# Hybrid decoder block on one core: first expert pair's loads written out, and expert weights loaded through two DMA queues

## The chip, the cores and the metric

The kernel runs on one core of one Trainium2 chip. The metric is the device time in microseconds of one execution. TensorE (PE in the profile) does the matrix products, VectorE (DVE) and ScalarE (ACT) the elementwise work, SyncE (SP) issues DMA transfers. An engine that can issue DMAs does so through a queue of its own: in the profile SP's transfers are queue q1 and ScalarE's are queue q10.

## The reference, cut to what matters

```python
def hybrid_layer(x, ...):
    xn = rms_norm(x, norm1_g)
    u, q, k, v, qi, ki, wi, gs, ga = split(xn @ w_in)
    y_ssm = s5_mixer(u, ...)                       # diagonal state space model, scan over 256 tokens
    y_att = dsa_attention(rope(q), rope(k), v, rope(qi), rope(ki), wi)   # 64 keys chosen for each token
    mixed = sigmoid(gs + b0) * (y_ssm @ w_proj_ssm) + sigmoid(ga + b1) * (y_att @ w_proj_attn)
    x = x + mixed @ w_out
    return x + moe(rms_norm(x, norm2_g), ...)

def moe(h, ...):                                   # 256 tokens, 32 experts, 4 chosen for each token
    gates = softmax over the top 4 of (h @ w_router + b_router), zero elsewhere
    for e in range(32):
        z = h @ w_moe_in[e] + b_moe_in[e]          # 1024 x 2048
        zg, zl = min(z[:, ::2], 7), clip(z[:, 1::2], -7, 7)
        act = zg * sigmoid(1.702 * zg) * (zl + 1)
        out += gates[:, e] * (act @ w_moe_out[e] + b_moe_out[e])   # 1024 x 1024
```

Everything is float32. The output is the RMS norm of the block's result.

## The kernel before

**Stages.** First the mixer: norm, the combined projection, the state space model, the attention, the projections and the residual. Then the head of the expert stage (router, places of the tokens, gates). Then 32 experts, one after the other. Each engine runs its own program; semaphores join them. The order on each engine is written out by hand.

**Mixer.** TensorE works through jobs (`JOBS`) of two 128-column tiles each (`feature_job`, the matmul of L1038). A job writes one of two rotating PSUM banks (`rot`, banks 0 and 1, by the parity of its number in `JOBS`), and a bank is free again when the job before last has been evicted (`rot_free`). The jobs P0_0 and P0_1 are the transposed probabilities of the first 128 tokens. Weights come in chunks of 1 MB through four slots (`wbuf`), loaded by SP. `mean_between` puts the matmul that sums the squares between the halves of job U0. `round_` is one of four rounds of the state space model on VectorE: four products that read the PSUM banks 4 to 7 (the last raises `bu_used`), two sums, eight scans, four more products. `score_job` writes the same banks 4 to 7; the first one waits for `bu_used` 4, `roped` 3 and copies of the keys. `choose_keys` finds the 64 largest scores in eight steps of eight.

**Experts.** An expert has 12 MB of weights, in six chunks of 2 MB (`NT`): chunks 0 to 3 (`NT_IN`) are its input weights, chunks 4 and 5 its output weights. SBUF holds two experts (`place_of(half, n)`), so expert e+2 takes the place of expert e, chunk by chunk. `chunk_used` counts the chunks that TensorE has finished; `moe_in[half][n]` says that a chunk has arrived.

TensorE's `body` for one expert, in order: input matmuls for k = 0 to 7 (L1326; two k for each chunk, a wait for the chunk at each even k; bias matmuls of L1337 after k = 0, and for the second expert the output bias of L1342), scatter of the expert before (L1302), gather for the next (L1285), transposes (L1351, L1355, L1293), output matmuls (L1366; a wait for chunk 4 at the start and for chunk 5 half-way). ScalarE evicts the output sums at L570 (`y_tok`) when `chunk_used` shows that the whole expert is done.

**Loads of the experts.** All go through SP. The first two experts are loaded during the mixer (`load_first`). From then on `one_pass` of SP reads the token count (`most_tokens`, waits for `flag_ok`) and runs a loop over pairs: for each chunk in the order 0 to 5 it waits until TensorE has used the same chunk of the expert two before, and issues the load (L373). Last comes the load of the final gain (L376, 0.5 MB). The output is stored from L381.

Of the kernel before, what the change touches and what calls it, by code (L numbers as in the profile page):

```python
# [21 lines left out]
T = 256  # L22
# [33 lines left out]
        "A0", "A1", "A2", "GLU0", "GLU1", "P0_0", "P0_1", "A3", "PS0", "PS1", "PS2",  # L56
# [15 lines left out]
def build(nc, io, out):  # L72
# [3 lines left out]
    with ExitStack() as ctx:  # L76
# [119 lines left out]
        u0_first, w_gain, tok_ok, rpart_ok, scaled_ok = [sem(n) for n in ("u0_first", "w_gain", "tok_ok", "rpart_ok", "scaled_ok")]  # L196
        x_in = [sem(f"x_in{n}") for n in range(2)]
# [6 lines left out]
        turned1, turned1_out = sem("turned1"), sem("turned1_out")  # L204
# [91 lines left out]
        def _(sp):  # L296
# [8 lines left out]
            def load_first(*pairs):  # L305
# [5 lines left out]
            sp.dma_start(wbuf[:, 0, 0:1024], io["w_mix"][0, :, 0:1024]).then_inc(u0_first, 16)  # L311
            sp.dma_start(x1[:, 4:8, :], io["x_t"][:, 4 * T:8 * T].rearrange("p (k t) -> p k t", k=4)).then_inc(
                x_in[1], 16)
# [49 lines left out]
            def one_pass(c, first, most_tokens=None):  # L363
                if most_tokens:
                    most_tokens()
                with sp.Fori(1 if isinstance(c, int) else 0, NE // 2) as m:
# [27 lines left out]
        def _(ac):  # L394
            ac.dma_start(x1[:, 0:4, :], io["x_t"][:, 0:4 * T].rearrange("p (k t) -> p k t", k=4)).then_inc(
                x_in[0], 16)
# [22 lines left out]
            for n in range(2):  # L419
                ac.wait_ge(x_in[n], 16)  # L420
# [73 lines left out]
            def prob_turned(t):  # L494
                for n in range(2 * (t + 1)):
                    if t:
                        ac.wait_ge(turned1, n + 1)
                        ac.activation(prob_t[:, 512 * n:512 * n + 512], ps[:, 4 + n, :], ACT.Copy).then_inc(
                            turned1_out, 1)
                    else:  # L500
                        evict(f"P0_{n}", prob_t[:, 512 * n:512 * n + 512], lambda b: b)
# [52 lines left out]
            def one_pass(c, first, most_tokens=None):  # L554
# [4 lines left out]
                def body(j, tail=False):  # L559
# [10 lines left out]
                    ac.activation(y_tok, ps[:, 2, :], ACT.Copy).then_inc(y_tok_ok, 1)  # L570
                gathered_rows(first)
                body(first)
                if most_tokens:
                    most_tokens()
                with ac.Fori(1, NE - 1) as e:
                    body(e + first)
                body(first + NE - 1, tail=True)
# [19 lines left out]
        def _(ve):  # L597
# [25 lines left out]
            for n in range(2):  # L623
                ve.wait_ge(x_in[n], 16)
                for k in range(4 * n, 4 * n + 4):
# [92 lines left out]
            def round_(i):  # L718
# [6 lines left out]
                tt(prod[3], bre, ei, ALU.mult).then_inc(bu_used, 1)  # L725
                ve.wait_ge(bu_used, i + 1)
# [38 lines left out]
            round_(0)  # L765
            round_(1)
            round_(2)
# [43 lines left out]
            def mask(t, first, end):  # L811
# [4 lines left out]
                if t:  # L816
                    ve.wait_ge(rot_done, JOB["P0_1"] + 1)
# [198 lines left out]
        def _(pe):  # L1016
# [28 lines left out]
            def mean_between(step):  # L1045
                if step == 1:
                    pe.wait_ge(ones_ok, 1)
                    pe.wait_ge(sq_sum, 1)
                    pe.matmul(ps[:, 2, 0:T], ones, squares[:, 0, :], start=True, stop=True).then_inc(mean_done, 1)
                    chunk_arrived(pe, "U0")  # L1050
# [486 lines left out]
```

## Time and profile before

| | |
|---|---|
| median of 3 runs | 1152.15 us (1150.76 to 1152.37) |
| the profiled execution | 1152.06 us |
| its span in the profile | 1150.3 us |
| PE busy | 1107.7 us, 96% |
| DVE busy | 342.5 us, 30% |
| ACT busy | 156.1 us, 14% |
| read from HBM | 435.52 MB |
| mean rate of the DMA engines over the span | 381 GB/s |
| mean granted TensorE clock | 0.998 of full |

A share of busy time is an average over stages that have different limits: VectorE is busy nine tenths or more of the mixer's first half and one tenth of the expert stage. So the view by slices of the span comes first, then the order of work in each stage. In the views, "x8" is a number of instructions, "[1.65 <-issue]" is the idle time before an instruction and what ended it, and each matmul call in float32 stands as two instructions. Times are from the start of the span.

### The profile page before, as it was taken

Reading aid. Unit: us, or ns where it says so; the run is one execution under the profiler, and the core shown is the slowest. Engines: PE = TensorE matmul, PEld = TensorE weight load, DVE = VectorE, ACT = ScalarE, POOL = GpSimd, SP = SyncE. Lnnn points to the kernel's source line nnn. Section 1 sums busy time; section 2 is a strip of 40 time slices with the busy share of each in tenths; the row PEclk is TensorE's granted clock in tenths of the full one; section 3 lists DMA queues with packets and bytes.
Section 4 is the critical chain, followed back from the end, with each engine's and each line's share of the span. In section 5 each row is a group of like instructions: output and inputs, shape, how many; then the busy total and the mean of one; then the engine's idle time right before and its main releaser. Section 6 shows DMA issues by size and latency. Waiting matters only on the chain.

```text
span 1150.3 us, 13793 instructions
## 1 busy us (share of the span) xinstructions
PE 1107.7 (96%) x5564; PEld 484.2 (42%) x5564; DVE 342.5 (30%) x761; ACT 156.1 (14%) x330; POOL 0.7 (0%) x8
## 2 busy tenths in 40 slices
PE   9999999999999999999999999999999999999996
PEld 7887788833333333333333333333333333333332
DVE  7999982121221211111111111111111111111112
ACT  2411361220101000010000000000000000000002
POOL 0000000000000000000000000000000000000000
PEclk9999999999999999999999999999999999999999
DMA  8344577769999999999999999999999999999995
GB/s 336 133 157 142 195 313 284 312 266 430 426 428 428 428 428 428 428 428 428 428 428 428 428 428 428 428 428 428 428 428 428 428 428 428 428 428 428 428 428 231
DMA packets 34010, 437.73 MB, mean 381 GB/s; under 512 B 4032, under 2 KB 4160, under 8 KB 6080
## 3 DMA queue, kind: packets, MB, share of 16 engines
q1 hardware_dynamic: 33840, 436.84, 90.5%
q10 hardware_dynamic: 144, 0.52, 0.2%
q8 instruction: 19, 0.31, 0.1%
q14 instruction: 7, 0.06, 0.0%
HBM read 435.52 MB, written 1.05 MB: 380 GB/s over the span
## 4 chain that ended last, share of the span: by engine, by line
PE 66%; DMA 17%; SPq 5%; DVE 2%; ACT 1%; issue 1%; another core or an unknown queue 0%; ACTq 0%; DVEq 0%
PE ps L1326 28%; DMA mem<-in_w_moe 17%; PE ps L1366 15%; PE ps L1038 6%; SPq L373 5%; PE ps L1302 4%; PE ps L1285 4%; PE ps L1251 2%; PE ps L1337 2%; PE ps L1216 1%; PE ps L1293 1%; PE ps L1351 1%; PE ps L1127 1%; PE ps L1355 0%; DVE late L606 0%
## 5 line engine op out<-in xcount | busy, mean ns | idle before, releaser
L1326 PE MATMUL ps<-mem,late 128*64 128x512 f32 x2048 | 459.0, 596 | 24.5 <-DMA mem<-in_w_moe 23.7
L1326 PEld LDWEIGHTS ps<-mem,late 128*64 128x64 f32 x2048 | 142.0, 137 | 332.8 <-issue 281.5
L972 DVE TENSOR_SCALAR late<-ps 128x512 f32<-128x512 f32 x32 | 22.1, 691 | 688.6 <-PE ps L1326 688.6
L1366 PE MATMUL ps<-mem,late 128*64 128x512 f32 x1024 | 226.8, 595 | 0.0
L1038 PE MATMUL ps<-mem 128*128 128x256 f32 x640 | 143.8, 382 | 0.9 <-ACT mem L452 0.9
L1038 PEld LDWEIGHTS ps<-mem 128*128 128x128 f32 x640 | 119.8, 190 | 21.8 <-issue 4.3
L1366 PEld LDWEIGHTS ps<-mem,late 128*64 128x64 f32 x1024 | 70.7, 137 | 133.3 <-issue 128.1
L561 ACT ACTIVATE late<-late 128x512 f32<-128x512 f32 x32 | 20.1, 630 | 514.9 <-DVE late L972 514.9
L1302 PE MATMUL ps<-late 64*128 64x512 f32 x256 | 63.6, 615 | 0.9 <-ACT late L570 0.9
L1285 PE MATMUL ps<-xs,late 128*64 128x512 f32 x256 | 61.9, 604 | 0.8 <-DVE late L606 0.8
L606 DVE TENSOR_TENSOR mem<-mem 128x1024 f32<-128x1024 f32 (+8 forms) x88 | 59.9, 722 | 1.3
L570 ACT ACTIVATE late<-ps 128x512 f32<-128x512 f32 x32 | 19.1, 597 | 229.3 <-PE ps L1366 229.3
L606 DVE TENSOR_TENSOR late<-late 128x128 f32<-128x128 f32 (+2 forms) x105 | 39.9, 406 | 12.1 <-ACT late L539 4.9
L1302 PEld LDWEIGHTS ps<-late 64*128 64x128 f32 x256 | 22.1, 186 | 41.9 <-issue 41.9
L1337 PE MATMUL ps<-bias_rows,late 32*64 32x512 f32 x256 | 35.1, 618 | 0.0
L1285 PEld LDWEIGHTS ps<-xs,late 128*64 128x64 f32 x256 | 15.7, 136 | 42.4 <-issue 41.5
L606 DVE TENSOR_TENSOR late<-ps,vec 128x512 f32<-128x512 f32 x32 | 22.1, 692 | 36.3 <-PE ps L1293 36.3
L606 DVE TENSOR_TENSOR mem<-ps,mem 128x1024 f32<-128x1024 f32 (+2 forms) x30 | 26.0, 898 | 21.3 <-PE ps L1038 12.0
L557 ACT ACTIVATE late<-ps 128x512 f32<-128x512 f32 x32 | 19.2, 599 | 73.9 <-PE ps L1285 73.9
L1251 PE MATMUL ps<-mem 128*128 128x256 f32 x128 | 28.8, 379 | 0.0
L1251 PEld LDWEIGHTS ps<-mem 128*128 128x128 f32 x128 | 24.0, 190 | 3.0
L1351 PEld LDWEIGHTS ps<-table,late 128*128 128x128 f32 x128 | 13.4, 140 | 28.1 <-issue 24.3
(153 smaller groups left out, 498.9 us busy)
## 6 DMA issues: line engine op xcount, KB each, us to landing
mem<-in_w_moe SPq DMA_DIRECT2D x192, 2048.0 KB, 41.2
mem<-in_w_mix SPq DMA_DIRECT2D x26, 1024.0 KB, 6.2
mem<-in_w_mix SPq DMA_DIRECT2D x2, 512.0 KB, 7.2
out<-xs SPq DMA_DIRECT2D x2, 512.0 KB, 3.1
mem<-mem SPq DMA_DIRECT2D x12, 64.0 KB, 2.0
late<-in_turn_w SPq DMA_DIRECT2D x1, 640.0 KB, 7.3
mem<-in_x_t ACTq DMA_DIRECT2D x1, 512.0 KB, 4.6
mem<-in_x_t SPq DMA_DIRECT2D x1, 512.0 KB, 7.3
```

Of the source, the lines that this page charges most:

```text
L373: sp.dma_start(place_of(half, n), expert_part(e, n)).then_inc(moe_in[half][n], 16)
L561: ac.activation(sig, gate_z, ACT.Sigmoid, scale=ALPHA).then_inc(sig_ok, 1)
L606: return ve.tensor_tensor(out_, a, b, op)
L972: ve.tensor_scalar(gate_z, z[:, 0], LIMIT, None, ALU.min).then_inc(z_gate, 1)
L1038: i = pe.matmul(b[:, m * T:m * T + T], slot[:, k, first_m + m, :], src[:, k, :], start=(k == 0), stop=(k == kt - 1))
L1251: i = pe.matmul(b[:, 0:T], wide(f"W{m // 2}")[:, k, m % 2, :], mixed[:, k, :], start=(k == 0), stop=(k == KD - 1))
L1285: i = pe.matmul(ps[64 * q:64 * q + SLOTS, 3, :], one_hot[:, t, :], xs[:, t, 512 * q:512 * q + 512], start=(t == 0), stop=(t == TT - 1))
L1302: i = pe.matmul(ps[:, 4 + 2 * t + q, :], gated_t[r, t * P:t * P + P], y_tok[r, :], start=False, stop=False, skip_group_check=True)
L1326: i = pe.matmul(ps[r, n // 2, :], h_sel[:, k % 4, k // 4, :], w[:, 512 * n:512 * n + 512], start=(k == 0), stop=(k == KD - 1))
L1337: pe.matmul(ps[r, n // 2, :], chosen[g, n, :], b_in[g, :], start=False, stop=False)
L1351: i = pe.transpose(ps[:, 0, n * P:n * P + P], act[:, n * P:n * P + P], ident)
L1366: i = pe.matmul(ps[64 * q:64 * q + SLOTS, 2, :], act_tile(k), w[:, 512 * q:512 * q + 512], start=(k == 0), stop=(k == KF - 1))
```

## The change

- **Expert loads on two queues.** SP loads only the input weights (chunks 0 to 3). ScalarE issues the two output chunks of expert e+2 at the end of its body for expert e, behind the eviction of `y_tok`.
- **Pairs written out.** SP's pair 1 (experts 2 and 3) is issued ahead of `most_tokens`; the loop runs over pairs 2 to 14; pair 15 is written out, and the last input chunk of the last expert comes as two DMAs of 1 MB, the second with a semaphore of its own (`last_in`), for which TensorE waits at k = 7.
- **Start.** The input x is loaded as four parts (three from ScalarE's queue) instead of two, the first 1024 columns of U0's weights as two parts. The sum of squares is multiplied one step later in job U0.
- **Mixer.** VectorE reads the last round's banks 4 to 7 ahead of the ropes of QI1 and QI3 (`round_inputs`), not behind them. The first score jobs wait for `roped` 2, not 3. The transposed probabilities of the first tokens go to banks 2 and 3 instead of two rotating jobs. ScalarE evicts gate A2 ahead of the exponentials. Six of the eight steps of the second `choose_keys`, not five, stand ahead of the first `probabilities`.
- **Head.** Three extra matmuls of 320 columns (`keep_clock`), whose result nobody reads, stand in front of three waits of TensorE.

```diff
+            def load_pair(m, last=False, parts=NT_IN):
                 for half in range(2):
-                        for n in range(NT):
+                    for n in range(parts):
                         e = 2 * m + half
                         sp.wait_ge(chunk_used, (e + first - 2) * NT + n + 1)
-                            sp.dma_start(place_of(half, n), expert_part(e, n)).then_inc(moe_in[half][n], 16)
+                        if last and half == 1 and n == NT_IN - 1:
+                            for i, arrived in enumerate((moe_in[half][n], last_in)):
+                                sp.dma_start(place_of(half, n)[:, SW * i:SW * i + SW],
+                                             expert_part(e, n)[:, SW * i:SW * i + SW]).then_inc(arrived, 16)
+                        else:
+                            sp.dma_start(place_of(half, n), expert_part(e, n)).then_inc(moe_in[half][n], 16)
+                if most_tokens:
+                    load_pair(1)
+                    most_tokens()
...
+                with sp.Fori(2 if isinstance(c, int) else 1, NE // 2 - 1) as m:
+                    load_pair(m)
+                load_pair(NE // 2 - 1, last=True)
...
                     ac.wait_ge(chunk_used, j * NT + NT)
                     ac.activation(y_tok, ps[:, 2, :], ACT.Copy).then_inc(y_tok_ok, 1)
+                    if isinstance(e, int) and e + 2 >= NE:
+                        return
+                    for n in range(NT_IN, NT):
+                        ac.dma_start(place_of(half, n), expert_part(e + 2, n)).then_inc(moe_in[half][n], 16)
...
-            for n in range(2):
-                ve.wait_ge(x_in[n], 16)
+            for n in range(4):
+                ve.wait_ge(x_in[n], 16)
...
             rope(kk.unsqueeze(1), 1, "KK")
+            round_inputs(3)
             rope(qi_t[:, 0:2], 2, "QI1")
             rope(qi_t[:, 2:4], 2, "QI3")
-            round_(3)
+            round_states(3)
...
             gate("A", gate_a, V_BG + KD, 1)
+            gate("A", gate_a, V_BG + KD, 2)
             ready(ACT.Exp)
             exponentials(0, 1, 0, NH)
-            gate("A", gate_a, V_BG + KD, 2)
...
-            choose_keys(1, 0, 5)
+            choose_keys(1, 0, 6)
             probabilities(0, 1, 0, NH)
-            choose_keys(1, 5, NSEL // 8)
+            choose_keys(1, 6, NSEL // 8)
...
-                    pe.wait_ge(roped, 3)
                     pe.wait_ge(bu_used, 4)
...
+                pe.wait_ge(roped, 2 + hg // 2)
...
                         pe.wait_ge(prob_ok, 1)
-                        b = job(f"P0_{n}")
+                        b = ps[:, 2 + n, :]
...
+            def keep_clock():
+
+                pe.matmul(ps[:, 1, 0:TB_ONE], ident, table[:, 0:TB_ONE], start=True, stop=True)
```

## Rows read from the trace of the kernel before

**Rows 1.** The page's 40 slices: VectorE busy in tenths, DMA rate.
```profile
DVE  7999982121221211111111111111111111111112
...
GB/s 336 133 157 142 195 313 284 312 266 430 426 428 428 428 428 428 428 428 428 428 428 428 428 428 428 428 428 428 428 428 428 428 428 428 428 428 428 428 428 231
```

**Rows 2.** Timeline of PE, the input matmuls of experts in mid-stage.
```profile
705.71 1.89 PE L1326 MATMUL ps<-mem,late 128*64 128x512 f32 x8
...
732.77 1.89 PE L1326 MATMUL ps<-mem,late 128*64 128x512 f32 x8
734.59 1.09 PE L1337 MATMUL ps<-bias_rows,late 32*64 32x512 f32 x8
735.61 12.24 PE L1326 MATMUL ps<-mem,late 128*64 128x512 f32 x56
```

**Rows 3.** Timeline of PE, the last experts.
```profile
1075.29 7.09 PE L1366 MATMUL ps<-mem,late 128*64 128x512 f32 x32
...
1104.65 7.09 PE L1366 MATMUL ps<-mem,late 128*64 128x512 f32 x32
...
1120.53 3.65 PE L1326 MATMUL ps<-mem,late 128*64 128x512 f32 x16 [0.75 <-DMA mem<-in_w_moe]
1125.42 3.65 PE L1326 MATMUL ps<-mem,late 128*64 128x512 f32 x16 [1.24 <-DMA mem<-in_w_moe]
...
1133.26 7.09 PE L1366 MATMUL ps<-mem,late 128*64 128x512 f32 x32
```

**Rows 4.** SP's issues at L373 in 250:252 us, with the time to landing.
```profile
L373 SPq DMA_DIRECT2D mem<-in_w_moe x1: 348/348/348, 250.1 to 250.1; - x1
DMA to landing us min/median/max: 9.0/9.0/9.0
```

**Rows 5.** Windows of 0.5 us: PE, PEld, DVE, ACT, POOL busy, granted clock, DMA share, GB/s.
```profile
244.00:244.50 0.50, 0.50 (x4) 0.12 (x2) 0.16 (x1) 0.00 (x0) 0.00 (x0) 0.50 0.09 33
...
247.50:248.00 0.50, 0.50 (x10) 0.06 (x3) 0.00 (x0) 0.00 (x0) 0.00 (x0) 1.00 0.00 0
```

**Rows 6.** Timeline of the head and the first expert.
```profile
238.64 1.94 PE L1285 MATMUL ps<-xs,late 128*64 128x512 f32 x8 [0.81 <-DVE late L606]
...
243.42 3.23 PE L1326 MATMUL ps<-mem,late 128*64 128x512 f32 x8 [0.78 <-DVE late L606]
246.58 1.43 PE L1337 MATMUL ps<-bias_rows,late 32*64 32x512 f32 x8
264.76 7.09 PE L1366 MATMUL ps<-mem,late 128*64 128x512 f32 x32
271.89 0.60 ACT L570 ACTIVATE late<-ps 128x512 f32<-128x512 f32 x1 [7.58 <-PE ps L1366]
```

**Rows 7.** DMA queues in 2.5:3 us, when both carry transfers: packets, MB, share.
```profile
q10 hardware_dynamic: 36, 0.15, 83.3%
q1 hardware_dynamic: 43, 0.02, 16.9%
```

**Rows 8.** Window of 5 us in the mixer, columns as in rows 5.
```profile
210.00:215.00 5.00, 5.00 (x26) 4.48 (x25) 0.65 (x2) 1.01 (x6) 0.00 (x0) 1.00 1.03 439
```

**Rows 9.** Timeline of the mixer: starts, idle times and what ended them.
```profile
8.95 1.14 DVE L626 TENSOR_SCALAR mem<-mem,vec 128x256 f32<-128x256 f32 x4 [1.92 <-DMA mem<-in_x_t]
13.06 0.67 PE L1049 MATMUL ps<-mem,table 128*128 128x256 f32 x2 [1.14 <-DVE mem L606]
...
113.88 0.73 PE L1127 MATMUL ps<-mem 32*128 32x128 f32 x16 [1.65 <-issue]
156.27 3.72 PE L1038 MATMUL ps<-mem 128*128 128x256 f32 x16 [0.89 <-ACT mem L452]
161.01 0.63 PE L1161 MATMUL ps<-table,xs 128*128 128x128 f32 x4 [0.58 <-ACT mem L517]
170.93 0.84 ACT L452 ACTIVATE mem<-ps,vec 128x256 f32<-128x256 f32 x2
172.14 0.69 DVE L606 TENSOR_TENSOR mem<-ps,mem 128x512 f32<-128x512 f32 x1 [0.71 <-PE ps L1038]
```

More of the change, by code:

```diff
@@ L55 @@
 JOBS = ["U0", "U1", "KK", "QI0", "QI1", "QI2", "QI3", "VW", "Q0", "Q1", "S0", "S1", "S2", "S3",
-        "A0", "A1", "A2", "GLU0", "GLU1", "P0_0", "P0_1", "A3", "PS0", "PS1", "PS2",
+        "A0", "A1", "A2", "GLU0", "GLU1", "A3", "PS0", "PS1", "PS2",
         "PS3"] + [f"W{m}" for m in range(KD)]
@@ L195, in build @@
             "vec_in", "tables_in", "consts_in", "b_blk_in", "c_raw_in", "rout_in", "bias_in", "gfin_in")]
-        u0_first, w_gain, tok_ok, rpart_ok, scaled_ok = [sem(n) for n in ("u0_first", "w_gain", "tok_ok", "rpart_ok", "scaled_ok")]
-        x_in = [sem(f"x_in{n}") for n in range(2)]
+        w_gain, tok_ok, rpart_ok, scaled_ok = [sem(n) for n in ("w_gain", "tok_ok", "rpart_ok", "scaled_ok")]
+        x_in = [sem(f"x_in{n}") for n in range(4)]
+        u0_first, last_in = [sem(f"u0_first{n}") for n in range(2)], sem("last_in")
         w_slot_in = [sem(f"w_slot_in{n}") for n in range(NBUF)]
@@ L394, in _ @@
         def _(ac):
[L395 to L396 removed]
+            for n in (0, 1, 3):
+                ac.dma_start(x1[:, 2 * n:2 * n + 2, :], io["x_t"][:, 2 * n * T:2 * n * T + 2 * T].rearrange(
+                    "p (k t) -> p k t", k=2)).then_inc(x_in[n], 16)
             chain = [0]
@@ L557, in gathered_rows, with body @@
                     ac.activation(h_tok, ps[:, 3, :], ACT.Copy).then_inc(h_tok_ok, 1)
-                def body(j, tail=False):
+                def body(j, e, half, tail=False):
                     ac.wait_ge(z_gate, j + 1)
@@ L570, in body @@
                     ac.activation(y_tok, ps[:, 2, :], ACT.Copy).then_inc(y_tok_ok, 1)
+                    if isinstance(e, int) and e + 2 >= NE:
+                        return
+                    for n in range(NT_IN, NT):
+                        ac.dma_start(place_of(half, n), expert_part(e + 2, n)).then_inc(moe_in[half][n], 16)
                 gathered_rows(first)
-                body(first)
+                body(first, 0, 0)
                 if most_tokens:
                     most_tokens()
-                with ac.Fori(1, NE - 1) as e:
-                    body(e + first)
-                body(first + NE - 1, tail=True)
+                body(first + 1, 1, 1)
+                with ac.Fori(1, NE // 2 - 1) as m:
+                    for half in range(2):
+                        body(2 * m + (first + half), 2 * m + half, half)
+                for half in range(2):
+                    body(first + NE - 2 + half, NE - 2 + half, half, tail=half == 1)
                 ac.wait_ge(first_sum_ok, c + 1)
@@ L622, in _ @@
             ve.tensor_scalar(pr(RED), pr(14), 3.1415925, -3.1415925, ALU.min, ALU.max).then_inc(par_v, 1)
-            for n in range(2):
+            for n in range(4):
                 ve.wait_ge(x_in[n], 16)
-                for k in range(4 * n, 4 * n + 4):
+                for k in range(2 * n, 2 * n + 2):
                     ve.tensor_scalar(x_g[:, k, :], x1[:, k, :], vec[:, V_G1 + k:V_G1 + k + 1], None,
@@ L764, in _ @@
             finish_phase(0)
-            round_(0)
-            round_(1)
-            round_(2)
+            for i in range(3):
+                round_inputs(i)
+                round_states(i)
             ve.wait_ge(consts_in, 16)
             rope(kk.unsqueeze(1), 1, "KK")
+            round_inputs(3)
             rope(qi_t[:, 0:2], 2, "QI1")
             rope(qi_t[:, 2:4], 2, "QI3")
-            round_(3)
+            round_states(3)
             rope(q_t, 2, "Q1", temps=[at(4 * SW + 1024 * n, 2, 2, T) for n in range(2)])
@@ L1045, in mean_between @@
             def mean_between(step):
+                if step == 0:
+                    pe.wait_ge(u0_first[1], 16)
                 if step == 1:
+                    chunk_arrived(pe, "U0")
+                if step == 2:
                     pe.wait_ge(ones_ok, 1)
@@ L1168, in attend @@
                 else:
-                    pe.wait_ge(*evicted("P0_0"))
-                    pe.wait_ge(*evicted("P0_1"))
+                    pe.wait_ge(turned0_out, 2)
                 for h in heads:
@@ L1322, in body @@
                             arrived(k // CH)
+                        if tail and k == KD - 1:
+                            pe.wait_ge(last_in, 16 * c + 16)
                         w = weights(k)
```

42 lines of the change are left out of this document (23 added, 19 removed).

## The prediction

> **What bounds the kernel now.** I read the rate of the DMA engines first [rows 1]: from the tenth slice (about 259 us) to the last but one it stands at 428 GB/s without a dip, while it wavers in the mixer. So in the expert stage the transfers never pause. Whether they also set the end is told by the timeline of TensorE. In mid-stage the input matmuls of one expert start 27.06 us after those of the expert before [rows 2]; the last experts stand 29.36 us apart and TensorE waits for w_moe twice in each [rows 3]. A chunk of 2 MB at 428 GB/s takes 4.89 us (the two waits of the last expert end 4.89 us apart, [rows 3]), six of them 29.36 us. TensorE is thus the faster of the two by 2.3 us per expert; the transfers fall behind, and at the end every expert costs what its six chunks cost. The end of the kernel is therefore: when the stream of chunks starts, plus 180 chunks of 4.89 us, plus what TensorE still has to do when the last ones land. Anything that starts the stream earlier is worth its full time; anything that lets it pause, or changes which chunk comes last, costs its full time.
>
> The stream starts when SP issues the first chunk of expert 2 at 250.1 us; it lands 9.0 us later, so 4.1 us lie around its 4.89 us of transfer [rows 4]. I put 1.5 us of them in front (no bytes move before 251 us) and 2.6 us behind.
>
> **Order of arrival, the largest term.** Before, one queue brings the chunks in the order in which TensorE wants them: 0 to 3, 4, 5. After, chunks 4 and 5 of expert e+2 are handed to the second queue at the end of expert e, and they need not queue behind the input chunks that are outstanding on SP's. What happens between two queues shows in the first microseconds, where both carry transfers: q10 moved 36 packets while q1 moved 43, though q10's were eight times as large [rows 7]. So the engines take packets from the two queues in turn. All packets of expert weights are equally large, so each queue gets half the rate while both have work.
>
> The Trainium skill says the same (page DMA: Bandwidth & Descriptors, section Queues, rings and completion order: an engine goes round robin over its queues, packet by packet), and the trace agrees as far as those 79 packets go.
>
> The two output chunks are thus fetched at once at half rate, though they are needed almost two experts later, and the input chunks that are needed next are delayed. In the long run that costs nothing: the engines stay busy, an expert still takes 29.36 us. It costs at the end, where input chunks are now last. Followed, with expert 29's end as zero:
> - An expert's TensorE time is 27.06 us. Its matmuls of k = 1 start 2.84 us in, and chunk 3 is wanted five sevenths of 12.2 later, at 11.5 [rows 2]; 15.5 us follow. With one expert per 29.36 us, chunk 3 of expert 30 lands at 29.36 - 15.5 = 13.8; its last byte comes 2.6 earlier, at 11.2.
> - Output chunks of expert 31 start at 2.2 (0.6 for the eviction of L570 [rows 6], 0.1 for the issue, 1.5 in front). By 11.2, at half rate, 4.5 of their 9.79 us of transfer are done, 5.3 are left.
> - Behind chunk 3 of expert 30 come four input chunks (19.6) and these 5.3: the last byte comes at 36.1 and lands at 38.7.
> - Expert 31 starts at 29.36 and no longer waits: it wants chunk 3 at 40.9. Its time is 15.0 for the input matmuls and 11.3 from there to its last output matmul (1129.07 to 1140.35, [rows 3]): it ends at 55.7, which is 17.0 us after the last landing.
>
> Before, chunk 3 of expert 31 ended a wait at 1125.42, chunks 4 and 5 landed 9.79 later at 1135.2, and the last output matmul ended at 1140.35 [rows 3], 5.15 us later. So the order costs 17.0 - 5.15 = **+11.9 us**. Splitting the last input chunk gives nothing, since TensorE does not wait for it. The end after the output matmuls (10 us) is the same; the gain row's load is last in both and has landed long before it is used.
>
> **The stream pauses once.** Before, chunk 4 of expert 0 is free half-way through L1366, at 268.3 [rows 6], ahead of the end of the four input chunks (251.4 + 19.6 = 271.0). After, both output chunks wait for the end of L1366 at 271.85 and 0.60 of eviction: they start at 272.45 + 0.1 + 1.5 = 274.1. SP has nothing to add, since expert 1 has not released a chunk. **+3.1 us**. One expert later the stream is full: 29.4 us of transfers against a shorter TensorE time. If the engines hid this the least is 0. ScalarE's two issues (0.35 us each, as in [rows 4]) stand in front of its sigmoid, which comes 17 us later: nothing waits.
>
> **The first pair ahead of the token count:** nothing. SP's first chunk waits for TensorE's first use at 249.9, not for the flag.
>
> **Clock.** At 244.0 the granted clock is 0.50, from 247.5 it is 1.00 again [rows 5], the lower of the two levels (1.2 and 2.4 GHz). TensorE had been idle three times for 0.8 us, twice of these in [rows 6]. The eight matmuls at 243.42 take 3.23 against 1.89, the bias matmuls 1.43 against 1.09 [rows 2, 6]: 1.7 us, all ahead of the first chunk's release. An added matmul of 320 columns takes about 0.58 us (eight calls of 256 columns take 3.72, [rows 9]), so it fills most of a gap and ends before what TensorE waits for. Bounds: 0 and -1.7. I take **-1.7**, since a quarter of each gap is left.
>
> **Mixer.** It shifts the stream one for one, but its waits are not additive. Waits of TensorE that the edits remove: 1.14 at the sum of squares, 1.65 at the first score job (it waited for VectorE's read of banks 4 to 7), 0.89 at GLU1 (gate A2 evicted behind the exponentials), 0.58 at the second transposes [rows 9], 4.3 us in all. What is late next: up to 100 us VectorE, at nine tenths or more [rows 1], paces both engines, so the 1.14 goes, and only an earlier arrival of x helps (it waited 1.92 us for it, [rows 9]); in four parts over two queues I give it 0.6, between 0 and 1.2. The 1.65, 0.89 and 0.58 bring TensorE forward to job A3; but job PS1 needs A3's bank, and ScalarE evicts A3 only after the second exponentials, at 170.93 to 171.77, whose pace VectorE sets. PS1 began at about 172.1 (VectorE's wait for PS0 ends there, [rows 9]), so 0.35 of these 3.1 us survive. The sixth step of `choose_keys` moves VectorE's work, it adds none. Sum **-0.95**; bounds 0 and -4.3.
>
> **Sum.** 1152.06 (the profiled execution, 0.1 under the median; its span is 1150.3) + 11.9 + 3.1 - 1.7 - 0.95 = **1164.4 us**.
>
> **Rivals.**
> - *Two queues move more than one* (chance 0.13). Against: in the shared microseconds nothing above the usual rate shows [rows 7]. For: a window of 5 us shows 439 GB/s [rows 8], 2.5% above 428. Both queues have work in 19.6 of 29.36 us, two thirds. 881 us x 2/3 x 2.5% = 14.7 us less: 1149.7 us, faster than before. It decides from 2.1% on, where it cancels the 12.3. A half of it gives 1157. The Trainium skill speaks against it (same page, Rules for kernel authors: spreading DMAs over issuing engines for bandwidth "Doesn't help"), and by it the time stays at the sum.
> - *No overtaking* (0.08): chunks are served in the order of issue, so input chunks are as early as before. Only +3.1, -1.7, -0.95: 1152.5 us, within. For: large transfers of both queues at once stand nowhere in the trace. Against: [rows 7].
> - *Sharing is uneven or costs rate* (0.13). If the second queue gets a third, its two chunks take the whole 29.36 us of an expert and TensorE comes to wait for chunk 5; the same reckoning gives about 4.5 us on top, 1169; at a fifth, 13 us, 1177. A loss of 1% of the rate gives 8.8 us, 1173.
> - *The mixer gains all its waits* (inside my case): -3.3 more, 1161. *The clock still falls:* 1166.1.
>
> **How the numbers follow.** My case has 0.66, from 1160.5 (all waits gained) to 1167.5 (clock and mixer give nothing, and an expert's parity in the last waits, 1 us). The range that holds 8 in 10 takes in the slower rival to 1171 and the half-sized gain in rate: 1154 to 1171. What this kernel's measurement can tell from no change is about 0.2%, 2.3 us. Faster than 1149.8: half of the first rival, 0.07. Within: the rest of what lies near, half of "no overtaking" and some of the first, 0.10. Slower: 0.83.
>
> **What the profile after would show.** Right: the first wait for a w_moe chunk far earlier than 773 us (about 580), at chunk 3 alone; ScalarE's chunks landing some 22 us after their issue; 428 GB/s throughout but for one dip at about 268 to 271 us; the last 17 us of TensorE's work without any transfer of weights; a granted clock of 1.00 around 241 us. Wrong: a rate above 437 GB/s while both queues have work, or ScalarE's chunks landing as late as SP's would have.

## The result, and the profile after

| | before | after |
|---|---|---|
| median | 1151.45 us (4 runs, 1150.63 to 1152.37) | 1166.24 us (4 runs, 1165.31 to 1169.06) |
| ratio | | 1.0131, 95% interval 1.0117 to 1.0146 |
| the profiled execution | 1152.06 us | 1169.06 us |
| its span | 1150.3 us | 1167.2 us |
| mean granted TensorE clock | 0.998 | 0.985 |

The changed kernel is slower by 1.3%. The prediction was 1164.4 us with a range of 1154 to 1171. The profiled execution is the slowest of the four of after; what may set it apart from the others, which were not traced, is taken up below (`queues_only`, `hold_clock`).

The page of after, its slices (40 of 29.2 us each), then the DMA queues (packets, MB, share of 16 engines), then two groups of instructions and of DMA issues:

```profile
PEclk9999999999999999999999999999999999999989
GB/s 332 137 153 136 217 319 259 309 325 396 425 429 429 427 428 431 427 427 431 427 427 431 429 426 430 430 427 428 431 427 428 431 427 428 430 430 426 428 389 37
...
q1 hardware_dynamic: 25488, 310.75, 63.8%
...
q10 hardware_dynamic: 9072, 126.62, 25.7%
...
L1361 PE MATMUL ps<-mem,late 128*64 128x512 f32 x2048 | 468.6, 609 | 31.3 <-DMA mem<-in_w_moe 31.1
...
mem<-in_w_moe SPq DMA_DIRECT2D x131, 2048.0 KB, 46.2
mem<-in_w_moe ACTq DMA_DIRECT2D x60, 2048.0 KB, 15.9
```

The rate is the same as in [rows 1]: 426 to 431 GB/s, no more with two queues than with one. ScalarE's 60 chunks land 15.9 us after their issue in the median, SP's after 46.2: the second queue is served without waiting for the first. (The 15.9 lies between two groups: from expert 6 on each chunk 4 takes 13.6 to 14.8 us, each chunk 5 22.9 to 24.1.) TensorE waits 31.1 us in all for w_moe, in its input matmuls alone. But the last slice but one falls to 389 and the last to 37, where before they had 428 and 231: at the end TensorE works with nothing left to load.

The timeline of TensorE after (start, duration, line, operation, tiles, instructions, idle time before it and what ended it), first three waits of twelve and then the last two experts:

```profile
582.79 3.65 PE L1361 MATMUL ps<-mem,late 128*64 128x512 f32 x16 [2.23 <-DMA mem<-in_w_moe]
...
612.15 5.35 PE L1361 MATMUL ps<-mem,late 128*64 128x512 f32 x16 [2.08 <-DMA mem<-in_w_moe]
...
671.52 5.09 PE L1361 MATMUL ps<-mem,late 128*64 128x512 f32 x16 [3.33 <-DMA mem<-in_w_moe]
...
1112.10 6.66 PE L1361 MATMUL ps<-mem,late 128*64 128x512 f32 x16 [3.33 <-DMA mem<-in_w_moe]
...
1130.75 1.89 PE L1361 MATMUL ps<-mem,late 128*64 128x512 f32 x8
...
1133.58 12.24 PE L1361 MATMUL ps<-mem,late 128*64 128x512 f32 x56
...
1150.01 7.09 PE L1401 MATMUL ps<-mem,late 128*64 128x512 f32 x32
```

The reader is to see four things. The first wait comes at 583 us, not at 773 as before. Each row with a wait has 16 instructions, the last two values of k, so the wait is at chunk 3 and nowhere else; the last expert has none, where before it had two [rows 3]. Nor does every expert wait: from the first wait to the last there are 19 experts and 12 waits. And the same 16 instructions take 3.65, 5.35, 5.09 or 6.66 us.

The end of the transfers, as stretches of 1 us (columns: stretch, its length, busy time of PE, PEld, DVE, ACT and POOL, granted clock, DMA share, GB/s):

```profile
1135.00:1136.00 1.00, 1.00 (x8) 0.35 (x6) 0.00 (x0) 0.00 (x0) 0.00 (x0) 1.00 0.50 193
1136.00:1137.00 1.00, 1.00 (x6) 0.29 (x4) 0.00 (x0) 0.00 (x0) 0.00 (x0) 1.00 0.19 78
1137.00:1138.00 1.00, 1.00 (x8) 0.36 (x6) 0.00 (x0) 0.00 (x0) 0.00 (x0) 1.00 0.00 0
```

No weights move after 1137. The last issue of a chunk, with its time to landing:

```profile
L376 SPq DMA_DIRECT2D mem<-in_w_moe x1: 433/433/433, 1085.6 to 1085.6; - x1
...
DMA to landing us min/median/max: 50.7/50.7/50.7
```

It lands at 1136.3, and the output matmuls end at 1157.1 (1150.01 + 7.09), 20.8 us later. Before, the last chunk landed at 1135.2 and they ended 5.2 us later. So the stream of chunks ends only 1.1 us later than before; nearly the whole loss lies between its end and the end of TensorE's work.

The queues from 900 to 905 us, when both have work:

```profile
q10 hardware_dynamic: 69, 1.13, 53.0%
q1 hardware_dynamic: 76, 1.02, 47.8%
```

Half each, now with large transfers on both sides; from 915 to 920 us q1 has the engines all but alone (148 packets, 2.15 MB).

The same stretches where the stream pauses after the change:

```profile
269.00:270.00 1.00, 1.00 (x8) 0.34 (x6) 0.00 (x0) 0.00 (x0) 0.00 (x0) 1.00 0.65 279
270.00:271.00 1.00, 1.00 (x6) 0.29 (x4) 0.00 (x0) 0.59 (x1) 0.00 (x0) 1.00 0.08 33
271.00:272.00 1.00, 1.00 (x6) 0.14 (x2) 0.00 (x0) 0.01 (x1) 0.00 (x0) 1.00 1.07 213
272.00:273.00 1.00, 1.00 (x10) 0.21 (x8) 0.00 (x0) 0.00 (x0) 0.00 (x0) 1.00 0.47 147
```

Against 428 GB/s these four lose 0.35 + 0.92 + 0.50 + 0.66 = 2.4 us of transfer. ScalarE's 0.59 in the second row is the eviction behind which the chunks are issued.

### The profile page after: what moved, and what is told of

Read it like the earlier page. It is cut to its first block, busy times and chain, and to the rows that moved or that the text cites. A ratio compares the mean times of both kernels' runs of the same rounds, so it can differ in the third digit from the quotient of the medians.

```text
span 1167.2 us, 13647 instructions
## 1 busy us (share of the span) xinstructions
PE 1119.0 (96%) x5570; PEld 489.4 (42%) x5570; DVE 342.3 (29%) x761; ACT 156.1 (13%) x330; POOL 0.7 (0%) x8
## 4 chain that ended last, share of the span: by engine, by line
PE 80%; DVE 7%; another core or an unknown queue 3%; ACT 1%; issue 1%; ACTq 0%
PE ps L1361 40%; PE ps L1401 19%; PE ps L1335 5%; PE ps L1318 5%; PE ps L1372 3%; PE ps L1279 2%; DVE mem L628 2%; PE ps L1386 2%; PE ps L1326 1%; PE ps L1244 1%; PE ps L1064 1%; DVE mem L815 1%; PE ps L1390 1%; DVE xs L628 1%
## 5 line engine op out<-in xcount | busy, mean ns | idle before, releaser
L1361 PE MATMUL ps<-mem,late 128*64 128x512 f32 x2048 | 468.6, 609 | 31.3 <-DMA mem<-in_w_moe 31.1
L1361 PEld LDWEIGHTS ps<-mem,late 128*64 128x64 f32 x2048 | 146.3, 140 | 345.3 <-issue 302.9
L1401 PE MATMUL ps<-mem,late 128*64 128x512 f32 x1024 | 226.8, 595 | 0.0
L1064 PEld LDWEIGHTS ps<-mem 128*128 128x128 f32 x640 | 119.8, 190 | 24.1 <-issue 5.7
L1401 PEld LDWEIGHTS ps<-mem,late 128*64 128x64 f32 x1024 | 70.7, 137 | 133.3 <-issue 128.1
L1318 PEld LDWEIGHTS ps<-xs,late 128*64 128x64 f32 x256 | 15.7, 136 | 42.2 <-issue 41.5
## 6 DMA issues: line engine op xcount, KB each, us to landing
mem<-in_w_moe SPq DMA_DIRECT2D x131, 2048.0 KB, 46.2
mem<-in_w_moe ACTq DMA_DIRECT2D x60, 2048.0 KB, 15.9
```

The costliest lines, as they stand in the source:

```text
L1064: i = pe.matmul(b[:, m * T:m * T + T], slot[:, k, first_m + m, :], src[:, k, :], start=(k == 0), stop=(k == kt - 1))
L1318: i = pe.matmul(ps[64 * q:64 * q + SLOTS, 3, :], one_hot[:, t, :], xs[:, t, 512 * q:512 * q + 512], start=(t == 0), stop=(t == TT - 1))
L1361: i = pe.matmul(ps[r, n // 2, :], h_sel[:, k % 4, k // 4, :], w[:, 512 * n:512 * n + 512], start=(k == 0), stop=(k == KD - 1))
L1401: i = pe.matmul(ps[64 * q:64 * q + SLOTS, 2, :], act_tile(k), w[:, 512 * q:512 * q + 512], start=(k == 0), stop=(k == KF - 1))
```

## The experiments

Every kernel below computes the whole result. Medians of the kernel before beside them: 1151.67 in the first group (`one_queue` to `tail_in_order`), 1151.66 in the second (`hold_clock` to `early_half`), 1151.1 in the third. A ratio is against that kernel. The three groups ran at different times, and the kernel before itself came out up to 0.6 us apart in them; so a difference of 0.3 or 0.4 us between kernels of different groups shows nothing by its time alone.

### one_queue: the changed kernel with all loads back on SP, in order

```diff
-                def load_pair(m, last=False, parts=NT_IN):
+                def load_pair(m, last=False, parts=NT):
...
-                    for n in range(NT_IN, NT):
-                        ac.dma_start(place_of(half, n), expert_part(e + 2, n)).then_inc(moe_in[half][n], 16)
```

> The changed kernel with the output weights back on SP's queue, in the order 0 to 5 and issued as TensorE releases each chunk; all other edits of the change stay (start, mixer, head, written-out pairs, split last input chunk). My theory (overtaking between the queues costs the time, the other edits give 1 to 2 us): about 1148.5 us, 3 us under the kernel before, of which 1.7 is the clock in the head and 1.4 the split last input chunk, which TensorE now does wait for. Rival (the other edits, or the many small transfers at the start, cost the time): over 1160.

Measured: 1149.08 us (1148.72 to 1149.40), ratio 0.9981, 0.9971 to 0.9990. The loss is gone, and the rest of the change is worth 2.6 us against the median of the kernel before. TensorE's last wait in its timeline:

```profile
1118.91 7.09 PE L1357 MATMUL ps<-mem,late 128*64 128x512 f32 x32 [0.62 <-DMA mem<-in_w_moe]
```

Thirty-two instructions in one row: chunks 2 and 3 of the last expert are multiplied with no wait between them. So the two queues cost 17.2 us of 1166.24, and the rival, that something else in the change is slow, falls.

### one_queue_late: one queue, but the output chunks issued as late as ScalarE issues them

```diff
+                            if n >= NT_IN:
+                                sp.wait_ge(y_tok_ok, e + first - 1)
+                            else:
+                                sp.wait_ge(chunk_used, (e + first - 2) * NT + n + 1)
```

> As one_queue, but SP issues chunks 4 and 5 only when the sums of the expert two before have been evicted, as late as ScalarE did, and behind the input chunks on one queue. It has the late issue without the overtaking. My theory: the stream pauses once for about 3 us and nothing else is lost, 1151.5 to 1152. Rival (the late issue is what costs): as slow as the changed kernel, 1166.

Measured: 1152.34 us (1151.82 to 1152.94), 3.3 above `one_queue`. The pause alone, with nothing overtaken; in its stretches of 2 us it stands in the place forecast:

```profile
270.00:272.00 2.00, 2.00 (x10) 0.43 (x6) 0.00 (x0) 0.60 (x1) 0.00 (x0) 1.00 0.04 16
272.00:274.00 2.00, 2.00 (x18) 0.52 (x16) 0.00 (x0) 0.00 (x0) 0.00 (x0) 1.00 1.03 254
```

One number shows the state of the stream: what the DMA engines moved from 246 to 274 us. It is 10.19 MB in `one_queue` and 8.91 here; 1.28 MB at 428 GB/s are 3.0 us, and the last chunk lands 3.2 us later. In after it is 9.16 MB: 2.4 us behind `one_queue`, which is the 2.4 of the four rows above; its last chunk lands 2.7 us later.

### queues_only: the kernel before with the two queues and nothing else

```diff
+                def load_pair(m, parts=NT_IN):
...
+                    for n in range(NT_IN, NT):
+                        ac.dma_start(place_of(half, n), expert_part(e + 2, n)).then_inc(moe_in[half][n], 16)
```

> The kernel before with nothing but the split of the expert loads over two queues (ScalarE issues chunks 4 and 5 behind its eviction). My theory: +11.9 for the order, +3.1 for the pause, and up to 3 us because TensorE's clock falls in the last long wait and its next matmuls run at half the rate: 1166.5 to 1170.5. Rival (the split alone is harmless and needs the rest of the change to hurt): about 1152.

Measured: 1166.95 us (1165.04 to 1171.34), ratio 1.0147, 1.0121 to 1.0173. The split by itself carries the whole loss. Its four times spread over 6 us, as those of after do over 4, where the ten of `one_queue` lie within 0.7. The profiled one is the fastest of the four; its timeline of TensorE, and its last chunk:

```profile
1082.38 5.35 PE L1340 MATMUL ps<-mem,late 128*64 128x512 f32 x16 [2.08 <-DMA mem<-in_w_moe]
...
1102.55 12.24 PE L1340 MATMUL ps<-mem,late 128*64 128x512 f32 x56
...
1129.61 12.24 PE L1340 MATMUL ps<-mem,late 128*64 128x512 f32 x56
...
1146.03 7.09 PE L1380 MATMUL ps<-mem,late 128*64 128x512 f32 x32
```
```profile
L374 SPq DMA_DIRECT2D mem<-in_w_moe x1: 333/333/333, 1087.9 to 1087.9; - x1
...
DMA to landing us min/median/max: 48.3/48.3/48.3
```

Its last wait is in expert 29; experts 30 and 31 run through. In after's profiled execution expert 30 still has a wait, and a long one. Here the last chunk lands at 1136.2, as in after, and the output matmuls end at 1153.1, 16.9 us later: the 17.0 that the prediction reckoned, where after has 20.8. Less the 5.2 of before, the order costs 11.8 us in this execution. That the other three, which were not traced, are slower for a late wait is likely, not shown.

### tail_in_order: two queues, but the last eight experts all on SP

```diff
+OWN = 24
...
-                with sp.Fori(2 if isinstance(c, int) else 1, NE // 2 - 1) as m:
+                with sp.Fori(2 if isinstance(c, int) else 1, OWN // 2) as m:
                     load_pair(m)
-                load_pair(NE // 2 - 1, last=True)
+                with sp.Fori(OWN // 2, NE // 2 - 1) as m:
+                    load_pair(m, parts=NT)
+                load_pair(NE // 2 - 1, last=True, parts=NT)
```

> The changed kernel, but from expert 24 on the output weights are loaded by SP in order; for experts 2 to 23 they stay on ScalarE's queue. My theory (sharing costs nothing while the stream is full, only the order at the end does): about 1152, although two queues carry 44 of the 60 output chunks. Rival (two queues at once move fewer bytes per us, or every expert pays): at least two thirds of the loss stays, 1161 or more.

Measured: 1151.75 us (1151.38 to 1152.61), ratio 1.0002, 0.9992 to 1.0011. Twenty-two experts have their chunks overtaken, TensorE waits at chunk 3 from 583 us on, and it costs nothing beyond the pause (2.7 above `one_queue`). The timeline has one more long wait and then none for 220 us; the end is that of one queue:

```profile
847.81 5.27 PE L1367 MATMUL ps<-mem,late 128*64 128x512 f32 x16 [3.31 <-DMA mem<-in_w_moe]
...
1067.46 3.65 PE L1367 MATMUL ps<-mem,late 128*64 128x512 f32 x16 [1.24 <-DMA mem<-in_w_moe]
...
1121.29 7.09 PE L1367 MATMUL ps<-mem,late 128*64 128x512 f32 x32 [0.62 <-DMA mem<-in_w_moe]
```

This is what tells the order at the end from sharing as such: if two queues lost rate, or if the waits of mid-stage cost time, most of the loss would have stayed.

### hold_clock: after, with six unread matmuls ahead of expert 30's wait

```diff
+                        if hold and k == KD - CH:
+                            pe.wait_ge(y_tok_ok, j)
+                            keep_busy(6, 2, table[:, 0:T])
```

> The changed kernel, and in expert 30 TensorE does six matmuls that nobody reads (2.6 us) while it waits for input chunk 3, its last wait. Theory (the matmuls behind that wait run at the lower clock, 6.66 us for the last two k where 3.65 are usual, and this lands on the end of the kernel): 3.0 us less than the changed kernel's 1166.2, about 1163.2, and 3.65 us for the last two k of expert 30. Rival (the slow stretch is not the idle time's doing, or is made up later): 1166.

Measured: 1166.11 us (1165.8 to 1167.5), no lower than after. In the timeline of one execution the place does what was expected of it:

```profile
1109.66 2.86 PE L1052 MATMUL ps<-table 128*128 128x256 f32 x12
1112.45 3.65 PE L1364 MATMUL ps<-mem,late 128*64 128x512 f32 x16
...
1128.10 1.89 PE L1364 MATMUL ps<-mem,late 128*64 128x512 f32 x8
```

The 16 instructions behind the wait take 3.65 us, not 6.66, and the last expert starts at 1128.10, not at 1130.75. The execution took 1166.15 against 1169.06. But the forecast of the median was a miss: the profiled execution of after is the slowest of four, the others took 1165.3 to 1167.0, and four runs of either kernel can't show more than that the top came down from 1169.1 to 1167.5. That the other executions of after have no long wait at expert 30 fits their times and was not seen in a trace of them; `queues_only`'s profiled execution is such a one. Two things speak for caution. In the same trace of `hold_clock` a wait of 3.37 us at 995 us, with no added matmul, was also followed by 3.65. And over whole executions the clock does not order the times: the two slower ones of after have a mean of 0.985, the two faster 0.987, and the slowest of `queues_only` has 0.983, the others 0.985 and 0.986; but the slowest of `hold_clock` has the highest, 0.990.

### no_keep_clock: one_queue without the three added matmuls of the head

```diff
-                pe.matmul(ps[:, 1, 0:TB_ONE], ident, table[:, 0:TB_ONE], start=True, stop=True)
+                pass
```

> one_queue without the three added matmuls in the head. Theory: the granted clock falls to 0.50 around 244 us as in the kernel before, the stream of chunks starts 1.7 us later and the whole kernel is 1.7 us slower than one_queue: 1150.8. Rival (the added matmuls only delay TensorE): 1149 or less.

Measured: 1149.47 us (1148.72 to 1150.90), 0.4 above `one_queue`, not 1.7. Its timeline shows the gaps open and the clock kept all the same:

```profile
243.40 1.94 PE L1357 MATMUL ps<-mem,late 128*64 128x512 f32 x8 [0.78 <-DVE late L624]
245.26 1.09 PE L1368 MATMUL ps<-bias_rows,late 32*64 32x512 f32 x8
```

The bias matmuls take 1.09, where [rows 6] has 1.43. The trace of `queues_only`, whose mixer and head are those of the kernel before without any change, shows the same: a gap of 0.79 us, then 1.94 and 1.09. So the fall of the clock that [rows 5] shows belongs to some executions only. The times agree: three of the ten are 1150.6 to 1150.9, the other seven 1148.7 to 1149.9. The kernel before falls apart likewise. Of its 25 executions in the first group twelve took 1149.9 to 1150.8 us at a mean granted clock of 0.998 or 0.999, twelve 1152.1 to 1153.8 at 0.996 to 0.998, and one 1151.7; the medians of the two dozens are 1.9 apart, and the profiled one, 1152.06, goes with the upper. The three matmuls are thus worth nearly 2 us in about half of the executions. Against the lower dozen (1150.45) `one_queue` gains 1.4 us, no more than the split of the last input chunk is worth (`no_split`).

### no_split: one_queue with the last input chunk as one DMA

```diff
-                load_pair(NE // 2 - 1, last=True)
+                load_pair(NE // 2 - 1)
...
-                        if tail and k == KD - 1:
-                            pe.wait_ge(last_in, 16 * c + 16)
```

> one_queue with the last input chunk of the last expert as one DMA of 2 MB. Theory: with one queue TensorE waits for that chunk, so it starts the last two k one half-chunk later; chunk 5's landing caps the gain of the split: +1.4 us, 1150.5. Rival (the split does nothing here either): 1149.1.

Measured: 1150.48 us (1149.81 to 1151.07), 1.4 above `one_queue` and 1.0 above `no_keep_clock` of its own group. In the timeline the second wait of the last expert is back:

```profile
1118.66 3.65 PE L1355 MATMUL ps<-mem,late 128*64 128x512 f32 x16 [0.71 <-DMA mem<-in_w_moe]
1123.54 3.65 PE L1355 MATMUL ps<-mem,late 128*64 128x512 f32 x16 [1.23 <-DMA mem<-in_w_moe]
```

From the last landing to the end of the output matmuls it is 5.2 us, as in the kernel before, and 3.7 in `one_queue`: by the traces the split is worth 1.5 us where input chunks come in order. With two queues TensorE does not wait for that chunk in the trace of after, so there it can give nothing.

### early_half: one_queue with the stream started 3.4 us earlier

The first chunk of expert 2 comes as two DMAs of 1 MB, the first behind k = 0; x comes in two parts and U0's first 1024 columns in one.

```diff
+                            if early and half == 0 and n == 0:
+                                sp.wait_ge(half_free, 1)
+                                sp.dma_start(place_of(0, 0)[:, 0:SW], expert_part(e, 0)[:, 0:SW]).then_inc(half_in, 16)
+                                sp.wait_ge(chunk_used, 1)
```

> one_queue with x and U0's first weights loaded in as many parts as before, and with the very first chunk of the stream (chunk 0 of expert 2) as two DMAs of 1 MB, the first issued when TensorE has used k = 0 of expert 0 and not k = 1. Theory (the stream's start is worth its full time at the end): 2.45 us from the earlier half chunk and 0.4 us because VectorE gets x at 8.95 and not at 9.36: 1146.2. Rival (another limit is near): under 1 us of gain.

Measured: 1149.49 us (1148.95 to 1150.26), 0.4 above `one_queue`: a miss. The stream does start early, but it pauses behind its first chunk and again for chunk 4:

```profile
246.00:248.00 2.00, 2.00 (x14) 0.77 (x12) 0.00 (x0) 0.00 (x0) 0.00 (x0) 1.00 0.92 266
...
252.00:254.00 2.00, 2.00 (x12) 0.72 (x10) 0.00 (x0) 0.00 (x0) 0.00 (x0) 1.00 0.94 234
...
268.00:270.00 2.00, 2.00 (x12) 0.71 (x10) 0.00 (x0) 0.03 (x1) 0.00 (x0) 1.00 0.86 303
```

Until 274 us it moved 10.67 MB against 10.19: of 3 us 1.1 are left. The next place is not free, since TensorE has not used it. Issue and time to landing, taken chunk by chunk from both traces, show where the rest goes: chunks 1 to 3 of expert 2 land 3.1 us ahead of those of `one_queue`, chunk 4 1.4 ahead, chunk 0 of expert 3 1.0, its chunk 2 0.7, and its chunk 5, at 311 us, 0.1. From there to 1089 us the lead stays at 0.1, and the last wait ends at 1119.01, that of `one_queue` at 1118.91. So the lead is gone after two experts. That chunk 4 was issued late is seen in the trace (at 266.53, 9.0 us before it landed, as with an empty queue in [rows 4]); what took the last 0.9 us stays open.

### late_start: one_queue with the stream started one chunk's use later

```diff
+                            if isinstance(e, int) and e == 2 and n == 0:
+                                sp.wait_ge(chunk_used, 2)
```

> one_queue, but SP issues the first chunk of the stream (chunk 0 of expert 2) only when TensorE has used chunk 1 of expert 0, one chunk later (3.5 us) than before. Theory (moving the stream's start later costs its full time, since the engines then stand still with work outstanding; moving it earlier gains only until the next chunk is not yet released, which is why early_half gained nothing): +3.5 us on one_queue's 1149.1, 1152.6. Rival (the start has slack both ways, and the end is set by the releases further on): under 1 us.

Measured: 1152.80 us (1152.17 to 1153.19), 3.7 above `one_queue`. The first issue comes 3.3 us later (251.8, not 248.5), and until 274 us 8.80 MB have moved, 3.2 us behind; from expert 3's chunk 4 (310 us) on the chunks land 3.8 us later. A later start costs its full time; together with `early_half` the two directions are not alike.

### x_two_parts: one_queue with x in two parts and U0's first weights in one, as before

```diff
-            for n in range(4):
+            for n in range(2):
                 ve.wait_ge(x_in[n], 16)
-                for k in range(2 * n, 2 * n + 2):
+                for k in range(4 * n, 4 * n + 4):
```

> one_queue with x loaded in two parts and U0's first weights in one, as in the kernel before. Theory: VectorE gets the last part of x at 8.95 instead of 9.36 us and everything behind it moves up by 0.4 us: 1148.7. Rival (early_half's lack of a gain comes from this part): 1149.5.

Measured: 1148.76 us (1148.24 to 1149.36), 0.3 below `one_queue`, ratio 0.9976, 0.9967 to 0.9985. It has the lowest median of all kernels run, but its lead over `one_queue` is about the spread of either, and the two stood in different groups: the times don't show it. The traces do: its first expert starts at 243.07, that of `one_queue` at 243.68, and its chunks land 0.3 us earlier from 311 to 1089 us. VectorE's timeline in it:

```profile
8.85 1.14 DVE L642 TENSOR_SCALAR mem<-mem,vec 128x256 f32<-128x256 f32 x4 [1.72 <-DMA mem<-in_x_t]
```

## Why the prediction was right, and where it was not

**What bounds the kernel, and the order of arrival (+11.9): right.** Each step has its row: packets of the two queues alternate, the rate stays, chunk 3 alone is waited for, from 583 us on (about 580 was forecast), of ScalarE's chunks each chunk 5 lands some 23 us after its issue (22 was forecast) and each chunk 4, which is ahead of it on the queue, some 14, and the last expert is TensorE's alone. `queues_only` shows that the split does it by itself, `one_queue` that without it nothing is lost, `tail_in_order` that it matters in the last experts only. The size is right too: in `queues_only`'s trace the last landing is 16.9 us ahead of the end of the output matmuls, 17.0 was reckoned. There is some luck in that. The reckoning gave each expert the same wait of 2.3 us; the traces have waits of 2.1 to 3.3 us in 12 experts of 19 and none in the others, and in which expert the last one falls moves the end by some us: the same stretch is 20.8 us in after, 3.0 of them for the clock, and 18.2 in `hold_clock`. The Trainium skill (page DMA: Bandwidth & Descriptors, section Queues, rings and completion order) has engines go round robin over their queues; by that rule the overtaking is expected, and the trace agrees with 69 and 76 packets in 5 us.

**The pause (+3.1): right, a little large.** After shows 2.4 us in its four rows; from the first issue to the last landing its stream takes 2.7 us more than that of before. The late issue alone cost 3.3 in time.

**The rivals fell.** Two queues move no more (426 to 431 GB/s after, 428 before); the chunks do overtake; the sharing is even and costs no rate (147 packets of q10 and 144 of q1 from 900 to 910 us).

**Head clock (-1.7): right in one execution, too large for the median.** In after the head runs at the full clock:

```profile
237.82 0.79 PE L1301 MATMUL ps<-table 128*128 128x320 f32 x2
...
243.58 1.94 PE L1361 MATMUL ps<-mem,late 128*64 128x512 f32 x8 [0.24 <-DVE late L628]
245.45 1.09 PE L1372 MATMUL ps<-bias_rows,late 32*64 32x512 f32 x8
```

The eight matmuls take 1.94 against 3.23 and the bias ones 1.09 against 1.43 [rows 6], 1.6 us. The failed step is that one profiled execution was taken for all of them: about half of the executions of before show the loss, and `no_keep_clock` is 0.4 above `one_queue` in the median.

**Mixer (-0.95): wrong.** The first expert starts at 243.58, 0.16 later than in [rows 6] and as good as in `queues_only`, which has the old mixer (243.55). All four waits of TensorE of [rows 9] are gone, 4.3 us, and three new ones stand in their place: 1.30, 1.27 and 1.73, again 4.3. Rows of VectorE and TensorE in the timeline of after:

```profile
8.34 0.62 DVE L648 TENSOR_SCALAR mem<-mem,vec 128x256 f32<-128x256 f32 x2 [1.81 <-DMA mem<-in_x_t]
...
24.37 7.15 PE L1064 MATMUL ps<-mem 128*128 128x256 f32 x32 [1.30 <-issue]
...
149.76 2.01 PE L1173 MATMUL ps<-mem 32*128 32x256 f32 x32 [1.27 <-DVE xs L844]
...
171.99 3.72 PE L1064 MATMUL ps<-mem 128*128 128x256 f32 x16 [1.73 <-ACT mem L469]
```

The 1.30 and the 1.27 were not foreseen. The last row is the wait that the prediction named as the next late one: PS1 waits 1.73 us for ScalarE to free A3's bank and starts at 171.99, as before (about 172.1). The step that failed is x: in four parts its first quarter is used at 8.34, but the next only at 9.36 with another 0.41 of waiting, and VectorE is through with it at 10.5, where two parts ended at 10.1 (8.95 + 1.14, [rows 9]). I gave 0.6 us to it; it costs 0.4. `x_two_parts` bears that out, with VectorE done at 9.99. So do all twelve traces together: the last part of x lands at 9.1 to 9.7 us in the eight with four parts and at 8.8 to 9.0 in the four with two, and the first expert starts 233.9 to 234.5 us after it in every one. From the end of VectorE's pass over x to that start it is 233.3 us in before and 233.1 in after and in `x_two_parts`: the other edits of the mixer gave 0.2 us, where 0.35 was counted on, and the later x took it back. (The runs with two parts also have U0's first weights in one, as before; the two are not told apart.)

**What the sum lacked: the clock behind a long wait, up to +3.0.** The last 16 instructions of an expert took 6.66 us behind the wait of 3.33 at 1112.10, and 3.65 where the clock stayed. In mid-stage that cost is paid while TensorE would wait anyway; at expert 30, the last that waits, it goes to the end. It is in the profiled execution in full and in `queues_only`'s not at all. That it is why the kernels with two queues to the end scatter over 4 to 6 us (`hold_clock` over 1.7) is likely and not shown.

The clock itself at that place, in stretches of 1 us of after (the granted clock stands behind the busy time of POOL):

```profile
1110.00:1111.00 1.00, 0.00 (x0) 0.00 (x0) 0.00 (x0) 0.00 (x0) 0.00 (x0) 1.00 1.08 459
1111.00:1112.00 1.00, 0.00 (x0) 0.00 (x0) 0.00 (x0) 0.00 (x0) 0.00 (x0) 0.68 0.88 377
1112.00:1113.00 1.00, 0.90 (x2) 0.30 (x4) 0.00 (x0) 0.00 (x0) 0.00 (x0) 0.50 1.08 459
...
1118.00:1119.00 1.00, 1.00 (x6) 0.30 (x4) 0.19 (x1) 0.00 (x0) 0.00 (x0) 0.90 1.11 475
```

TensorE stands still in the first two rows; the clock falls to 0.50, the lower of its two levels, and returns in the last.

**The account** of the profiled executions, 1169.06 - 1152.06 = 17.0, can be taken from the traces in four stretches. The first issue of the stream comes at 248.44 and not at 250.08, 1.6 us earlier (head clock -1.8, mixer +0.2; -2.65 was forecast). From there to the last landing it takes 2.7 us more (the pause, +3.1 forecast). From the last landing to the end of the output matmuls it is 20.8 us and not 5.2, 15.7 more (+11.9 forecast); 3.0 of them are the clock behind the last wait. The end behind it is 0.2 longer. So 0.8 us of the order's stretch are left, within the 1 us that was set aside for where in an expert the last waits fall; no run separates them. Against the medians the change cost 14.8, and the forecast was 12.3 above the profiled execution of before, which is one of the slower of its kind. It was right since its largest term was; of the misses in this account the clock (3.0), the mixer (1.1) and what is left of the order (0.8) made it slower than forecast, and the pause alone, by 0.4, went the other way, so it was not right because its errors cancelled.

**Two sentences were wrong as they stood.** "Anything that starts the stream earlier is worth its full time": `late_start` paid its full 3.7 us, but of the 3.1 us by which `early_half`'s chunks were ahead at first 0.1 was left by 311 us. Up to `one_queue` an earlier start is kept: its first issue is 1.5 us ahead of before, and its chunks land 1.5 to 1.7 us ahead from 257 to 1121 us. Beyond it, little is: in `x_two_parts` TensorE's first expert starts 0.6 us earlier still, its chunks land 0.7 us ahead at first and 0.3 from 311 us on. And that splitting the last input chunk gives nothing holds only beside the second queue; with one it gives 1.4 to 1.5 us.

## What to carry to other kernels

Where one queue is saturated and brings its transfers in the order of need, look at the order before the rate: here a second queue added no bandwidth (428 GB/s either way) and handed half of it to whatever stood in it, and the bill came at the end, when what was delayed was last. Putting the last eight experts back in order took all of it away but the pause; that only what is needed at once should go on a second queue follows from this, but no run tried it. An earlier start of such a stream helps only as far as the next places are free, so look at what is released next before counting on it. And where the end hangs on what lands last, take the time from the last landing to the end of the work from both traces: it shows the loss at once (5.2 against 20.8 us).

## What the runs showed of the hardware that was not expected

- TensorE's clock can fall over a single wait for a transfer: in after, behind the four waits of 3.3 us the next 16 matmul instructions took 5.0 to 6.7 us instead of 3.65, behind the four of 2.1 us 5.35, and behind the four of 2.2 to 2.4 us the full-speed 3.65. In the four traces with such waits together (after, `queues_only`, `tail_in_order`, `hold_clock`) the clock fell at 16 of 17 waits of 3.1 us or more, at 12 of 13 of 2.1 us, and at none of seven of 2.2 to 2.4 us. In after it fell to 0.50 before the long waits were over (at 671.1 us, where the wait ended at 671.5), and 0.6 to 0.9 us after the end of those of 2.1 us (at 613.0 us, where the wait ended at 612.15). Why some cost clock and others not stays open; length alone does not decide. The mean granted clock of the kernel went from 0.998 to 0.985 with twelve such waits. Six unread matmuls in one gap came with the full clock (3.65), which is one case.
- The same gaps of 0.8 us lowered the clock to 0.50 in one execution (before, 244 us) and left it at 1.00 in another (`queues_only`, 244 us), without any change to the code there. A term of this kind taken from one trace has to be weighed by how often it happens.
- Two large streams on two queues share the 16 engines evenly and lose nothing (428 GB/s from 280 to 1130 us with one queue and with two).
- x in four smaller transfers over two queues was complete for VectorE 0.4 us later than in two (its last part landed at 9.1 to 9.7 us in eight traces, at 8.8 to 9.0 in four).
